# Six instead of four seven-product pairs in three of the four down projections, with half of the weight sums made by adding transfers

## The chip, the cores and the metric

The kernel runs on one core of a Trainium2 chip. The metric is the device time of one execution in microseconds (us), as the median of three runs.

## The reference

A two-block network on 256 tokens of width 1024 in fp32. The first block has four feed-forward layers (two per depth), a state-space mixer (SSD), a neighbourhood attention and two gated embeddings; the second has three attentions and a wide MLP. The change touches the feed-forward layers:

```python
def swiglu(x, w_gu, w_down):
    g, u = jnp.split(x @ w_gu, 2, axis=-1)
    return (jax.nn.silu(g) * u) @ w_down          # (256 x 2816) @ (2816 x 1024)

for i in range(DEPTH):                            # DEPTH = 2
    h = h + 0.5 * swiglu(rmsnorm(h, ffn1_norm[i]), ffn1_w_gu[i], ffn1_w_down[i])
    h = h + mixer_i(rmsnorm(h, mix_norm[i]))      # i = 0: SSD, i = 1: neighbourhood attention
    h = h + 0.5 * swiglu(rmsnorm(h, ffn2_norm[i]), ffn2_w_gu[i], ffn2_w_down[i])
    gate = jax.nn.sigmoid(rmsnorm(h, ple_norm[i]) @ ple_w_gate[i])
    h = h + gate * rmsnorm(p[i] @ ple_w_proj[i], ple_post_norm[i])
```

## The kernel before, in words

**Products.** Every fp32 operand is split into a high part and a low rest (`whi`, `wlo` of the weights, `aThi`, `aTlo` of the activations), and a product of two blocks is three matmuls: high by high, high by low, low by high. A matmul of the down projection takes a stationary 128 x 128 block (128 tokens, 128 of the 2816 inner features) and streams 512 weight columns. So the 22 feature blocks, two token halves and two column halves cost 22 x 4 x 3 matmuls if all is done plainly.

**Pairs.** Two feature blocks, two token halves and two column halves are eight block products. For a *pair* (feature blocks 2j and 2j+1) the kernel does them with seven (a Strassen-like scheme with sums of weight blocks and differences of activation blocks): 21 matmuls instead of 24. Before, each of the four layers (i = 0 to 3) has four pairs, j = 0 to 3 (`PAIRS`, line 21).

**Tiles.** Weights come in tiles, and a plan (`plan_of`, with `down_tiles` for the order of the down projection) lists them in the order in which all engines take them. In this document the tiles of a down projection are called:

- **P**j, label `paired`: two feature blocks by 1024 columns, loaded (1 MB); 1536 of its 2048 columns per partition are split, and TensorE does 9 matmuls with it;
- **M**j, label `mixed`: the four sums of weight blocks (2048 columns), not loaded; VectorE makes them out of the raw tile of P (`sums`: one addition over 1024 columns, then two over 512, each of which needs the last), and TensorE does 12 matmuls;
- **R**0, R1, ...: a `rest` tile, done plainly: four feature blocks of one column half, 24 matmuls, or two (1024 columns, 12 matmuls);
- **L**0, L1, L2: the last three tiles (24, 24 and 12 matmuls).

Before, the order is R0 P0 M0 R1 P1 M1 R2 P2 M2 R3 P3 M3 R4 L0 L1 L2; R4 is a short one. The 22 tiles of the up projection, two for each of 11 chunks c, come ahead of it.

**The ring of a tile.** SyncE loads it into one of four raw slots (`NRAW`), when the tile four loads before has been split. ScalarE writes `whi` (line 1546), VectorE then `wlo` (line 2130), into one of three slots (`NSPL`): tile n can be split only when TensorE has released tile n-3. TensorE takes tile n (`take`) when its `whi` and its `wlo` are there. `whi` of an M tile waits for the last of its sums. All engines follow one program order; VectorE's order in the down projection is sums of P, `wlo` of P, `wlo` of M, `wlo` of the next tile (`ahead`).

**Activations.** After up chunk c, TensorE turns its result (line 628), ScalarE copies it (`araw`, `aThi`), and for c below `PAIRS` GpSimd makes the differences (`differences`, line 2790: `dsum`, three operations); ScalarE and VectorE split them into `dThi` and `dTlo`. GpSimd has little else to do: reciprocal roots, a few additions of `h`, sums in the SSD mixer. It issues no transfer.

Of the kernel before, what the change touches and what calls it, by code (L numbers as in the profile page):

```python
# [20 lines left out]
PAIRS = 4  # L21
# [141 lines left out]
def plan_of(dr):  # L163
    p = Plan()

    def ffn(i, up, down, extra=None):
# [6 lines left out]
        def rest(c, y):  # L173
            k0, nk = DOWN_TILES[c, y]
            p.add(("down", i, c, y), [wsrc(down, k0, nk, c * 512, 512)], nk, 512)

        for what, x in DOWN_ORDER:
# [5 lines left out]
        for x in DOWN_LAST:  # L183
            rest(*x)
# [78 lines left out]
DOWN_ORDER, DOWN_TILES, DOWN_LAST = down_tiles(PAIRS)  # L263
# [130 lines left out]
def programs(dr, mem, banks, plan, ev):  # L394
# [33 lines left out]
    def landed(n):  # L428

        if labels[n][0] == "mixed":  # L430
            return at("tsum", *labels[n][1:])
        return at(f"d_w{plan.raw_of[n] % NRAW}", n)

    def dTlo(c):
        return mem["dTlo"][:, c, :, :]
# [117 lines left out]
    def sync(S):  # L553
# [67 lines left out]
    def tensor(T):  # L621
# [203 lines left out]
        def mixed_down(i, r, turn_last):  # L825
# [17 lines left out]
            def rest(c, y):  # L843
                k0, nk = DOWN_TILES[c, y]
# [10 lines left out]
            def seven(j):  # L855
                first, final = j == 0, j == PAIRS - 1
# [19 lines left out]
            for what, x in DOWN_ORDER[1:]:  # L876
# [6 lines left out]
            closing_block([("down", i) + DOWN_LAST[0]], (6, 7), aThi, aTlo, DOWN_TILES[DOWN_LAST[0]][0])  # L883
            residual_in(r, 0, (6, 7))
            held, k0 = [], DOWN_TILES[DOWN_LAST[1]][0]
            for x in DOWN_LAST[1:]:
                hi, lo = take("down", i, *x)
                held += [(hi[:, k, :], lo[:, k, :]) for k in range(DOWN_TILES[x][1])]
            T.wait_ge(*at("aTlo", i, 10))
            for t in range(2):  # L890
                for k, (hi, lo) in enumerate(held):
# [7 lines left out]
                    if t and k == DOWN_TILES[DOWN_LAST[1]][1] - 1:  # L899
                        last.then_inc(*sig(*named(("down", i) + DOWN_LAST[1])))  # L900
                last.then_inc(*sig(*half(("down", i) + DOWN_LAST[2], t)))
# [637 lines left out]
    def scalar(A):  # L1539
# [71 lines left out]
        def ffn(i, r, extra=None):  # L1611
            fa, aThi = mem["fa"], mem["aThi"]

            def high_a(c):
                A.wait_ge(*at("turn_a", i, c))
                b = banks[4 + c % 2]
                if c >= PAIRS:
# [15 lines left out]
            def mixed_down(r):  # L1633
                take("down", i, 0, 0)
                high_a(10)
                for what, x in DOWN_ORDER[1:]:
# [14 lines left out]
                take("down", i, *DOWN_LAST[2])  # L1651
# [6 lines left out]
            for c in range(11):  # L1658
# [15 lines left out]
                if 1 <= c <= PAIRS:  # L1674
# [451 lines left out]
    def vector(V):  # L2126
# [8 lines left out]
        def sums(n):  # L2135
# [9 lines left out]
            else:  # L2145
                V.wait_ge(*at("dTlo", i, PAIRS - 1))
# [914 lines left out]
```

## Time and profile before

| | |
|---|---|
| median of three runs | 1669.83 us (1669.68 to 1669.99) |
| the profiled execution | 1669.54 us |
| its span (first to last instruction) | 1667.7 us |
| TensorE (PE) busy | 1655.8 us, 99% |
| VectorE (DVE) busy | 1161.4 us, 70% |
| ScalarE (ACT) busy | 940.5 us, 56% |
| GpSimd (POOL) busy | 125.1 us, 8% |
| transfers | 300.58 MB, mean 180 GB/s |

The profiler's span is 1.84 us shorter than the time of the same execution; differences between two spans can be added to the time as they are. "Busy" is an average over stages; whether VectorE is early or late for one tile is read from a timeline. A matmul's duration in a row is the time from its start to the end of its pipeline, so the pace of TensorE is read from starts, or from a piece of the chain divided by its matmuls.

### The profile page before, as it was taken

How to read it: one execution, taken by the hardware profiler on the slowest of the kernel's cores; microseconds unless marked ns; L12 is line 12 of the kernel's file. 1: busy time of each engine (PE TensorE's matmuls, PEld its weight loads, DVE VectorE, ACT ScalarE, POOL GpSimd, SP SyncE). 2: the span in 40 equal slices, each digit the busy share in tenths (PEclk: the TensorE clock that was granted, in tenths of full speed). 3: DMA queues.
4: the chain of work that ended last, by engine and by line, in shares of the span. 5: the costliest groups of instructions: out<-in, count | busy, mean ns of one | idle time of the engine just before them, and what ended most of it. 6: DMA issues, size and time to landing. Idle time of an engine off the chain costs nothing.

```text
span 1667.7 us, 23289 instructions
## 1 busy us (share of the span) xinstructions
PE 1655.8 (99%) x9318; PEld 1416.7 (85%) x9318; DVE 1161.4 (70%) x1500; ACT 940.5 (56%) x1363; POOL 125.1 (8%) x135
## 2 busy tenths in 40 slices
PE   8999999999999999999999999999999999999998
PEld 7888899999788888888888778888889999988886
DVE  5657878999966568765688767567855578776643
ACT  6545566777865445754456666545653556564532
POOL 0100000000111000010007401000000000000000
PEclk9999999999999999999999999999999999999999
DMA  9654677676556646656487336655655533465551
GB/s 302 194 183 164 186 187 208 180 196 207 161 190 197 195 158 204 200 178 194 159 228 244 114 111 205 190 184 163 220 182 165 161 102 127 156 210 178 177 195 57
DMA packets 244235, 300.58 MB, mean 180 GB/s; under 512 B 9505, under 2 KB 175777, under 8 KB 244129
## 3 DMA queue, kind: packets, MB, share of 16 engines
q1 hardware_dynamic: 238480, 289.26, 54.6%
q10 hardware_dynamic: 5648, 9.85, 2.4%
q8 instruction: 74, 1.21, 0.3%
q14 instruction: 33, 0.26, 0.0%
HBM read 297.96 MB, written 1.11 MB: 179 GB/s over the span
## 4 chain that ended last, share of the span: by engine, by line
PE 98%; DVE 1%; DMA 0%; ACT 0%; issue 0%; DVEq 0%; ACTq 0%
PE bank L625 95%; PE bank L628 4%; DMA prm<-in_prm 0%; DVE wlo L2130 0%; ACT hThi L1546 0%; DVE rTlo L2133 0%; DVE hTlo L2133 0%; DVE xn L2133 0%; DVE h L2133 0%; ACT rThi L1546 0%; DVE xn L2200 0%; DVEq L2988 0%; ACT xn L1543 0%; ACT whi L1546 0%; ACTq L2086 0%
## 5 line engine op out<-in xcount | busy, mean ns | idle before, releaser
L2130 DVE TENSOR_TENSOR wlo<-raw,whi 128x2048 fp32r<-128x2048 f32 (+2 forms) x284 | 613.5, 2165 | 231.1 <-ACT whi L1546 231.1
L1546 ACT ACTIVATE whi<-raw 128x2048 fp32r<-128x2048 f32 (+2 forms) x284 | 511.7, 1810 | 167.1 <-PE bank L625 162.7
L625 PE MATMUL bank<-whi,hThi 128*128 128x512 f32 x1056 | 420.8, 398 | 0.5 <-ACT whi L1546 0.5
L625 PE MATMUL bank<-wlo,hThi 128*128 128x512 f32 x1056 | 412.4, 390 | 0.4 <-DVE wlo L2130 0.4
L625 PE MATMUL bank<-whi,hTlo 128*128 128x512 f32 x1056 | 396.9, 391 | 0.0
L625 PE MATMUL bank<-hThi,whi 128*128 128x256 f32 x888 | 253.4, 285 | 0.0
L625 PE MATMUL bank<-hThi,wlo 128*128 128x256 f32 x888 | 251.2, 283 | 0.0
L625 PE MATMUL bank<-hTlo,whi 128*128 128x256 f32 x888 | 251.2, 283 | 0.0
L625 PEld LDWEIGHTS bank<-whi,hThi 128*128 128x128 f32 x1056 | 198.8, 188 | 44.8 <-issue 5.8
L625 PEld LDWEIGHTS bank<-whi,hTlo 128*128 128x128 f32 x1056 | 198.6, 188 | 42.4
L625 PEld LDWEIGHTS bank<-wlo,hThi 128*128 128x128 f32 x1056 | 198.8, 188 | 40.3 <-DVE wlo L2130 1.5
L625 PEld LDWEIGHTS bank<-hThi,whi 128*128 128x128 f32 x888 | 169.5, 191 | 3.8 <-issue 3.3
L625 PEld LDWEIGHTS bank<-hTlo,whi 128*128 128x128 f32 x888 | 169.5, 191 | 0.2
L625 PEld LDWEIGHTS bank<-hThi,wlo 128*128 128x128 f32 x888 | 169.5, 191 | 0.2
L625 PE MATMUL bank<-whi,aThi 128*128 128x512 f32 x288 | 113.6, 395 | 0.4
L625 PE MATMUL bank<-whi,aTlo 128*128 128x512 f32 x288 | 112.2, 390 | 0.0
L625 PE MATMUL bank<-wlo,aThi 128*128 128x512 f32 x288 | 112.1, 389 | 0.0
L1543 ACT ACTIVATE ftmp<-bank,st 128x256 f32<-128x256 f32 x88 | 41.5, 476 | 101.5 <-PE bank L625 101.5
L2130 DVE TENSOR_TENSOR aTlo<-bank,aThi 128x512 fp32r<-128x512 f32 (+2 forms) x60 | 29.3, 511 | 78.5 <-ACT aThi L1546 78.5
L1546 ACT ACTIVATE aThi<-bank 128x512 fp32r<-128x512 f32 (+2 forms) x60 | 25.5, 457 | 98.3 <-PE bank L628 98.3
L2790 POOL TENSOR_TENSOR st<-st,cst 128x1 f32<-128x1 f32 (+2 forms) x35 | 36.9, 1068 | 458.6 <-DVE st L2173 433.5
L1546 ACT ACTIVATE hThi<-bank,prm 128x128 fp32r<-128x128 f32 (+1 forms) x152 | 43.4, 379 | 47.5 <-PE bank L628 42.4
(245 smaller groups left out, 2157.0 us busy)
## 6 DMA issues: line engine op xcount, KB each, us to landing
raw<-in_ffn_w_gu SPq DMA_DIRECT2D x172, 512.0 KB, 4.8
raw<-in_w_in SPq DMA_DIRECT2D x30, 1024.0 KB, 5.1
raw<-in_ffn_w_down SPq DMA_DIRECT2D x24, 1024.0 KB, 5.1
raw<-in_ffn_w_down SPq DMA_DIRECT2D x40, 512.0 KB, 4.0
raw<-in_ssd_w_in SPq DMA_DIRECT2D x16, 1024.0 KB, 5.7
raw<-in_ssd_w_in SPq DMA_DIRECT2D x32, 512.0 KB, 5.6
raw<-in_w_up SPq DMA_DIRECT2D x16, 1024.0 KB, 5.4
raw<-in_w_down SPq DMA_DIRECT2D x16, 1024.0 KB, 5.1
```

Source lines behind the costliest of these rows:

```text
L625: return T.e.matmul(out, lhsT, rhs, start=start, stop=stop, skip_group_check=skip)
L628: return T.e.transpose(out, in_, ident)
L1543: return e.activation(out, in_, func, **kw)
L1546: return e.activation(out, in_, ACT.Identity, **kw)
L2130: return e.tensor_tensor(out, a, b, op)
L2790: return e.tensor_tensor(out, a, b, op)
```

## The change

- Layers i = 1, 2, 3 get six pairs; layer 0 keeps four. For six pairs `down_tiles` gives the order R0 P0 M0 R1 P1 M1 R2 P2 M2 P3 M3 P4 M4 P5 M5 L0 L1 L2, where R2 is the short one (12 matmuls): four pairs stand directly behind each other.
- For the pairs 1, 3 and 5 of these layers (`AHEAD`), VectorE makes no sums. M1, M3 and M5 are loaded from a DRAM buffer `mix` (1 MB each) through a raw slot of their own, and P1, P3 and P5 load three quarters (0.75 MB), without the block that only the sums need.
- `mix` is filled by 54 transfers (nine tiles of six steps) on GpSimd's queue, from DRAM to DRAM: three of six copy, three add (`accum_op`). They move 512 KB (steps 0 and 1) or 256 KB each. Each waits for the one before (`m_step`) and for a weight tile's `whi` (`mix_at`), so at most one is under way. They are set one per up chunk (two tiles) in the feed-forward layers and one per two projection tiles in the SSD mixer. None is issued in a down projection.
- The differences are made for six chunks in these layers; `dTlo` is cut in two buffers.

```diff
--- before.py
+++ after.py
@@ -18,7 +18,11 @@
-PAIRS = 4
+PAIRS = (4, 6, 6, 6)
+AHEAD = ((), (1, 3, 5), (1, 3, 5), (1, 3, 5))
+BEATS = (range(1, 11), range(11), range(10), range(10))
+SSD_BEATS = (1, 29, 2)
+MIX = [(i, j) for i in range(4) for j in AHEAD[i]]
@@ plan_of: the mixed tile of a pair in AHEAD now has a source in DRAM
-                p.add(("mixed", i, x), None, 4, 512)
+                p.add(("mixed", i, x), [dr["mix"][i, x]] if x in AHEAD[i] else None, 4, 512)
@@ each layer has an order of its own
-DOWN_ORDER, DOWN_TILES, DOWN_LAST = down_tiles(PAIRS)
+DOWN_ORDER, DOWN_TILES, DOWN_LAST = zip(*(down_tiles(n) for n in PAIRS))
...
+    def summed_here(n):
+        return labels[n][0] == "mixed" and labels[n][2] not in AHEAD[labels[n][1]]
...
@@ sync, load(n)
-                if labels[m][0] == "paired":
+                if labels[m][0] == "paired" and summed_here(m + 1):
                     S.wait_ge(*at("tsum", *labels[m][1:]))
+            if labels[n][0] == "paired" and not summed_here(n + 1):
+                e.dma_start(slot[:, 1:2, 0:512], pieces[0][:, 1:2, :]).then_inc(*sig(f"d_w{q % NRAW}", n, by=16))
+                e.dma_start(slot[:, :, 512:1024], pieces[1]).then_inc(*sig(f"d_w{q % NRAW}", n, by=16))
+                return
+            if labels[n][0] == "mixed":
+                S.wait_ge(*at("m_step", *labels[n][1:], 5))
...
@@ vector, ahead(m)
-                if labels[n][0] == "paired":
+                if labels[n][0] == "paired" and summed_here(n + 1):
                     sums(n)
...
@@ gpsimd
+        def mix(i, j, step):
+
+            w = dr["ffn1_w_down" if i % 2 == 0 else "ffn2_w_down"][i // 2]
+            block = lambda k, c: w[256 * j + 128 * k:256 * j + 128 * k + 128, 512 * c:512 * c + 512].unsqueeze(1)
+            first = block(0, 0)
+            diagonal = bass.AP(first.tensor, first.offset, [[D, P], [P * D + 512, 2], [1, 512]])
+            target = dr["mix"][i, j]
+            if step == 0:
+                done = e.dma_start(target[:, 0:2, :], block(0, 1).to_broadcast([P, 2, 512]))
+            elif step == 1:
+                done = e.dma_start(target[:, 0:2, :], diagonal, accum_op=ALU.add)
+            elif step == 2:
+                done = e.dma_start(target[:, 2:3, :], target[:, 0:1, :])
+            elif step == 3:
+                done = e.dma_start(target[:, 2:3, :], block(1, 1), accum_op=ALU.add)
+            elif step == 4:
+                done = e.dma_start(target[:, 3:4, :], target[:, 2:3, :])
+            else:
+                done = e.dma_start(target[:, 3:4, :], block(1, 0), accum_op=ALU.add)
+            done.then_inc(*sig("m_step", i, j, step, by=16))
+
+        steps = [(i, j, step) for i, j in MIX for step in range(6)]
+        beats = iter(range(len(steps)))
+
+        def mix_at(n):
+
+            b = next(beats, None)
+            if b is not None:
+                G.wait_ge(*at("w_hi", n))
+                if b:
+                    G.wait_ge(*at("m_step", *steps[b - 1]))
+                mix(*steps[b])
+
         def ffn(i, extra=None):
-            for c in range(PAIRS):
-                differences(i, c)
+
+            for c in range(11):
+                if c < PAIRS[i]:
+                    differences(i, c)
                 if c == 2 and extra is not None:
                     ple_rstd(extra)
+                if c in BEATS[i]:
+                    mix_at(tile["up", i, c, 0])
...
         rstds(1)
+        for k in range(*SSD_BEATS):
+            mix_at(tile[SSD_TILES[k]])
         ssd()
...
@@ layout and build
-    put("dThi", [P, PAIRS, 3, P], F32R, a0)
-    put("dTlo", [P, PAIRS, 3, P], F32R, z + 56 * 1024)
+    put("dThi", [P, 7, 3, P], F32R, a0)
+    put("dTloA", [P, 5, 3, P], F32R, z + 56 * 1024)
+    put("dTloB", [P, 2, 3, P], F32R, z + 72 * 1024)
...
+    dr["mix"] = nc.dram_tensor("mix", (4, 7, P, 4, 512), F32, kind="Internal").ap()
```

VectorE, the down projection of layer i = 1, before, from `aTlo` of the last chunk on. `wlo<-raw` over 2048 columns is an R tile, over 1536 a P tile, over 1024 a short R tile; `ts` are the sums, and `wlo<-ts` is an M tile.

```order
L2130 TENSOR_TENSOR wlo<-raw,whi 128x2048 [waits s_w_hi]
L2130 TENSOR_TENSOR ts_75<-raw 128x1024 [waits s_w_rel,s_d_w2]
L2130 TENSOR_TENSOR ts_75<-ts_75,raw 128x512 [waits s_v_sums] x2
L2130 TENSOR_TENSOR wlo<-raw,whi 128x1536 [waits s_w_hi]
L2130 TENSOR_TENSOR wlo<-ts_75,whi 128x2048 [waits s_w_hi]
L2130 TENSOR_TENSOR wlo<-raw,whi 128x2048 [waits s_w_hi]
L2130 TENSOR_TENSOR ts_76<-raw 128x1024 [waits s_d_w0]
L2130 TENSOR_TENSOR ts_76<-ts_76,raw 128x512 [waits s_v_sums] x2
L2130 TENSOR_TENSOR wlo<-raw,whi 128x1536 [waits s_w_hi]
L2130 TENSOR_TENSOR wlo<-ts_76,whi 128x2048 [waits s_w_hi]
```

The same engine and layer of the changed kernel, from R2 (1024 columns) to P5; M3 is `wlo<-raw` over 2048 columns now:

```order
L2143 TENSOR_TENSOR wlo<-raw,whi 128x1024 [waits s_w_hi]
L2143 TENSOR_TENSOR ts_76<-raw 128x1024 [waits s_w_rel,s_d_w1]
L2143 TENSOR_TENSOR ts_76<-ts_76,raw 128x512 [waits s_v_sums] x2
L2143 TENSOR_TENSOR wlo<-raw,whi 128x1536 [waits s_w_hi]
L2143 TENSOR_TENSOR wlo<-ts_76,whi 128x2048 [waits s_w_hi]
L2143 TENSOR_TENSOR wlo<-raw,whi 128x1536 [waits s_w_hi]
L2143 TENSOR_TENSOR wlo<-raw,whi 128x2048 [waits s_w_hi]
L2143 TENSOR_TENSOR ts_75<-raw 128x1024 [waits s_w_lo,s_d_w0]
L2143 TENSOR_TENSOR ts_75<-ts_75,raw 128x512 [waits s_v_sums] x2
L2143 TENSOR_TENSOR wlo<-raw,whi 128x1536 [waits s_w_hi]
L2143 TENSOR_TENSOR wlo<-ts_75,whi 128x2048 [waits s_w_hi]
L2143 TENSOR_TENSOR wlo<-raw,whi 128x1536 [waits s_w_hi]
```

Between the sums of P2 and those of P4 stand four `wlo`, of P2, M2, P3 and M3, and no R tile; before, an R tile stood between any two pairs.

GpSimd in the up projection of layer i = 1, before: differences of the chunks 1 and 2 and two roots.

```order
L2790 TENSOR_TENSOR dsum<-araw 128x256 [waits s_araw]
L2790 TENSOR_TENSOR dsum<-araw,dsum 128x128 [waits s_g_differences] x2
L2790 TENSOR_TENSOR dsum<-araw 128x256 [waits s_dTlo,s_araw]
L2790 TENSOR_TENSOR dsum<-araw,dsum 128x128 [waits s_g_differences] x2
L2790 TENSOR_TENSOR st<-st,cst 128x1 [waits s_v_gates] x2
```

And now:

```order
L2803 TENSOR_TENSOR dsum<-araw 128x256 [waits s_araw]
L2803 TENSOR_TENSOR dsum<-araw,dsum 128x128 [waits s_g_differences] x2
L2896 DMA mix<-in_ffn_w_down 128x2x512 [waits s_m_step,s_w_hi]
L2803 TENSOR_TENSOR dsum<-araw 128x256 [waits s_dTlo,s_araw]
L2803 TENSOR_TENSOR dsum<-araw,dsum 128x128 [waits s_g_differences] x2
L2803 TENSOR_TENSOR st<-st,cst 128x1 [waits s_v_gates] x2
L2898 DMA mix<-mix 128x512 [waits s_m_step,s_w_hi]
```

A step, with its wait for the step before, now stands between the differences of two chunks.

## Rows read from the trace of the kernel before

**Rows 1.** The page: span, busy time, and the chain that ended last, by engine

```profile
span 1667.7 us, 23289 instructions
...
PE 1655.8 (99%) x9318; PEld 1416.7 (85%) x9318; DVE 1161.4 (70%) x1500; ACT 940.5 (56%) x1363; POOL 125.1 (8%) x135
...
PE 98%; DVE 1%; DMA 0%; ACT 0%; issue 0%; DVEq 0%; ACTq 0%
```

**Rows 2.** The chain in order of time (start, us, piece), down projections of i=1 and 3

```profile
597.70 10.93 PE bank L625 x48
...
609.07 4.79 PE bank L625 x21
...
613.98 41.13 PE bank L625 x180
...
1132.28 41.09 PE bank L625 x180
```

**Rows 3.** TensorE's timeline (start, us, instruction) at the start of R1, i=1

```profile
613.98 0.47 PE L625 MATMUL bank<-whi,aThi 128*128 128x512 f32 x1
614.29 0.39 PE L625 MATMUL bank<-wlo,aThi 128*128 128x512 f32 x1
```

**Rows 4.** VectorE's timeline, down projection of i=1: R1, P1, M1, R2, R4

```profile
611.54 2.29 DVE L2130 TENSOR_TENSOR wlo<-raw,whi 128x2048 fp32r<-128x2048 f32 x1 [1.11 <-ACT whi L1546]
613.75 1.22 DVE L2130 TENSOR_TENSOR ts<-raw 128x1024 f32<-128x1024 f32 x1
615.00 1.42 DVE L2130 TENSOR_TENSOR ts<-ts,raw 128x512 f32<-128x512 f32 x2
616.34 1.75 DVE L2130 TENSOR_TENSOR wlo<-raw,whi 128x1536 fp32r<-128x1536 f32 x1
618.41 2.29 DVE L2130 TENSOR_TENSOR wlo<-ts,whi 128x2048 fp32r<-128x2048 f32 x1 [0.32 <-ACT whi L1546]
621.75 2.29 DVE L2130 TENSOR_TENSOR wlo<-raw,whi 128x2048 fp32r<-128x2048 f32 x1 [1.05 <-ACT whi L1546]
...
641.34 1.23 DVE L2130 TENSOR_TENSOR wlo<-raw,whi 128x1024 fp32r<-128x1024 f32 x1 [0.20 <-ACT whi L1546]
```

**Rows 5.** ScalarE's timeline in the same down projection: M1, then R2 with P2, R4

```profile
616.45 1.92 ACT L1546 ACTIVATE whi<-ts 128x2048 fp32r<-128x2048 f32 x1 [3.57 <-DVE ts L2130]
619.80 3.54 ACT L1546 ACTIVATE whi<-raw 128x2048 fp32r<-128x2048 f32 x2 [1.43 <-PE bank L625]
...
640.25 1.06 ACT L1546 ACTIVATE whi<-raw 128x1024 fp32r<-128x1024 f32 x1 [1.43 <-PE bank L625]
```

**Rows 6.** Transfers: issues by line, KB each, median us from issue to landing

```profile
raw<-in_ffn_w_down SPq DMA_DIRECT2D x24, 1024.0 KB, 5.1
...
cum<-ct ACTq DMA_DIRECT2D x1, 64.0 KB, 2.4
```

**Rows 7.** Loads into raw, two in a row (649 to 651 us)

```profile
L570 SPq DMA_DIRECT2D raw<-in_ple_w_gate x2: 367/368/368, 649.3 to 650.5; - x2
...
DMA to landing us min/median/max: 5.0/5.9/6.8
```

**Rows 8.** Stretches: window, us, busy by engine, clock, DMA share, GB/s

```profile
645.00:650.00 5.00, 5.00 (x24) 4.14 (x23) 4.57 (x3) 3.46 (x3) 0.00 (x0) 1.00 0.83 290
...
360.00:404.00 44.00, 44.00 (x365) 42.94 (x364) 43.09 (x70) 31.48 (x52) 0.00 (x0) 1.00 0.63 195
```

**Rows 9.** GpSimd's timeline in up chunks of i=1

```profile
507.50 0.73 POOL L2790 TENSOR_TENSOR dsum<-araw 128x256 f32<-128x256 f32 x1 [12.24 <-ACT araw L1546]
508.32 1.01 POOL L2790 TENSOR_TENSOR dsum<-araw,dsum 128x128 f32<-128x128 f32 x2
518.87 0.74 POOL L2790 TENSOR_TENSOR dsum<-araw 128x256 f32<-128x256 f32 x1 [9.55 <-ACT araw L1546]
```

**Rows 10.** ScalarE's timeline there: the differences are taken

```profile
512.69 0.30 ACT L1546 ACTIVATE aThi<-dsum 128x128 fp32r<-128x128 f32 x1
```

**Rows 11.** VectorE on xTs and gate (min/median/max ns), SSD stage

```profile
L2130 DVE TENSOR_TENSOR xTs<-xTs,gate x8: 691/692/884, 298.3 to 459.9; 128x512 f32<-128x512 f32 x8
```

More of the change, by code:

```diff
@@ L173, in rest @@
         def rest(c, y):
-            k0, nk = DOWN_TILES[c, y]
+            k0, nk = DOWN_TILES[i][c, y]
             p.add(("down", i, c, y), [wsrc(down, k0, nk, c * 512, 512)], nk, 512)
-        for what, x in DOWN_ORDER:
+        for what, x in DOWN_ORDER[i]:
             if what == "rest":
@@ L434, in dTlo @@
     def dTlo(c):
-        return mem["dTlo"][:, c, :, :]
+        return mem["dTloA"][:, c, :, :] if c < 5 else mem["dTloB"][:, c - 5, :, :]
     def rstd(r, t):
@@ L875, in mixed_down @@
             clear(0, 1, 2, 3, 5)
-            for what, x in DOWN_ORDER[1:]:
+            for what, x in DOWN_ORDER[i][1:]:
                 if what == "rest":
@@ L898, in mixed_down @@
                         turn(1, 0, 1)
-                    if t and k == DOWN_TILES[DOWN_LAST[1]][1] - 1:
-                        last.then_inc(*sig(*named(("down", i) + DOWN_LAST[1])))
-                last.then_inc(*sig(*half(("down", i) + DOWN_LAST[2], t)))
+                    if t and k == DOWN_TILES[i][DOWN_LAST[i][1]][1] - 1:
+                        last.then_inc(*sig(*named(("down", i) + DOWN_LAST[i][1])))
+                last.then_inc(*sig(*half(("down", i) + DOWN_LAST[i][2], t)))
             residual_in(r, 1, (2, 3))
@@ L1635, in mixed_down @@
                 high_a(10)
-                for what, x in DOWN_ORDER[1:]:
+                for what, x in DOWN_ORDER[i][1:]:
                     if what == "rest":
@@ L1650, in mixed_down @@
                     high(1, 0, 1)
-                take("down", i, *DOWN_LAST[2])
+                take("down", i, *DOWN_LAST[i][2])
                 if r == 1:
@@ L2253, in mixed_down @@
                 low_a(10)
-                for what, x in DOWN_ORDER[1:]:
+                for what, x in DOWN_ORDER[i][1:]:
                     if what == "rest":
@@ L2259, in mixed_down @@
                     take("mixed", i, x)
-                take("down", i, *DOWN_LAST[0])
+                take("down", i, *DOWN_LAST[i][0])
                 merged()
@@ L2263, in mixed_down @@
                 for t in range(2):
-                    residual(r, t, 0, half(("down", i) + DOWN_LAST[0], t), 6 + t, 0.5)
-                take("down", i, *DOWN_LAST[1])
+                    residual(r, t, 0, half(("down", i) + DOWN_LAST[i][0], t), 6 + t, 0.5)
+                take("down", i, *DOWN_LAST[i][1])
                 early_quarters(r)
@@ L2268, in mixed_down @@
                 for t in range(2):
-                    residual(r, t, 1, half(("down", i) + DOWN_LAST[2], t), 2 + t, 0.5)
+                    residual(r, t, 1, half(("down", i) + DOWN_LAST[i][2], t), 2 + t, 0.5)
                     if r == 1 and t == 0:
@@ L2274, in mixed_down @@
                     scaled(0)
-                take("down", i, *DOWN_LAST[2])
+                take("down", i, *DOWN_LAST[i][2])
                 if r == 1:
@@ L2896, in gpsimd @@
         ffn(3, 1)
+        assert next(beats, None) is None
         rstds(7)
```

38 lines of the change are left out of this document (19 added, 19 removed).

## The prediction

> **What bounds the kernel now.** I read the page first: the span is 1667.7 us, TensorE is busy for 1655.8 us of it, and the chain that ended last is TensorE's to 98% [rows 1]. So matmuls that go are worth their full time, unless TensorE waits for something in their place. Then the chain in order of time, at the down projection of layer i = 1. 48 matmuls over 512 columns take 10.93 us, so one takes 0.2277 us: P 2.05 us, M 2.73, a pair 4.78 (the row says 4.79 for 21), R 5.46, a short R 2.73. R0 and the first pair end at 613.86, and from 613.98 on 180 matmuls follow without a gap; in layer 3 the same [rows 2]. Last, VectorE's and ScalarE's timelines there, for the steps that lead from a released slot to the next tile:
>
> - release to `whi`: R1 begins at 613.98, ends 5.46 later at 619.44, and ScalarE begins R2's `whi` at 619.80: 0.36 us [rows 2, 5];
> - `whi` over 2048 columns 1.92 us, and VectorE begins 0.04 after it ends (616.45 + 1.92 = 618.37, then 618.41) [rows 4, 5];
> - `wlo` over 2048 columns: 2.29 to its end, 2.21 to the next start (611.54 to 613.75); over 1536 columns 1.75; sums: 2.59 to the next start (613.75 to 616.34), their last ends 0.08 after that (615.00 + 1.42), and M's `whi` begins 0.03 later [rows 4, 5];
> - `wlo` ended to TensorE started: 613.83 to 613.98, 0.15 us [rows 3, 4].
>
> A tile over 2048 columns thus needs 0.36 + 1.92 + 0.04 + 2.29 + 0.15 = 4.76 us from the release of the slot three tiles back, and TensorE spends 4.78 us on the two tiles between when these are a P and an M. R2 shows it: ready at 621.75 + 2.29 + 0.15 = 624.19, wanted at 619.44 + 4.78 = 624.22. The down projection runs without a gap, but with 0.03 us to spare; one rest tile between two pairs (5.46 us) is what lets VectorE catch up with the sums.
>
> **The change part by part.**
>
> *Removed matmuls.* Two more pairs in three layers, three matmuls less for each: 6 x 3 x 0.2277 = 4.10 us off TensorE's path.
>
> *VectorE where four pairs stand together (P2 to M5).* TensorE needs 4 x 4.78 = 19.1 us. VectorE needs 2.59 + 1.75 + 2.21 = 6.55 for a pair that it sums and 3.96 for one that is loaded, 21.0 together. It is short by 1.9 us, in spite of the loaded sums. Tile by tile:
>
> - M2: from R1's release 0.36 + 1.06 (`whi` over 1024 [rows 5]) + 0.03 + 1.15 (the short `wlo`, 1.23 to its end [rows 4], less the same 0.08 overlap) + 2.67 (sums) + 0.03 + 1.92 + 0.04 + 2.29 + 0.15 = 9.70; TensorE has P1, M1, R2 and P2, 9.56. It waits 0.14.
> - M3: 4.76 against M2 and P3, 4.78. No wait.
> - P4: its sums stand on VectorE behind `wlo` of M3, which waits for the release of P2. So 0.36 + 1.92 + 0.04 + 2.21 + 2.59 + 1.75 + 0.15 = 9.02, against M2, P3 and M3, 7.51: 1.51, of which M2's wait has taken 0.14. It waits 1.37. Queued behind these sums are `wlo` of P4 and M4, and TensorE wants both.
> - M4: counted from the start of P4's `wlo`: 0.08 + 0.03 + 1.92 + 0.04 + 2.29 + 0.15 = 4.51, and TensorE comes at 1.75 + 0.15 + 2.05 = 3.95. It waits 0.56.
> - P5, M5, L0: P5 is loaded and has 1 us to spare; M5 and L0 are the 4.76 against 4.78. No wait.
>
> 2.07 us per down projection, near the 1.9 of the balance; three give 6.21. A wait also breaks the stream: R1's second matmul comes 0.31 after its first instead of 0.23 [rows 3]. Nine restarts at 0.08 are 0.7 us. R1's own wait is there now too.
>
> *Loads.* A pair with loaded sums fetches 1.75 MB. From the issue of P2's load (R1 just split) to the `whi` of L0 the queue must bring 6.5 MB (6.8 million bytes). TensorE spends 5.46 + 4.78 + 2.73 + 3 x 4.78 and 2.07 of waits on the way, 29.4 us, 29.9 with the two handovers; less the fixed part of a load (5.1 less 3.0, below) 27.8 remain: 245 GB/s is needed. Two loads issued at 649.3 and 650.5 landed 5.0 and 6.8 us later, so 3.0 us apart: 350 GB/s [rows 7]; a 5 us stretch shows 290 [rows 8]. The tightest is P2: issued at 613.83 in R1's terms, landed 5.1 later [rows 6], wanted by its sums at 619.44 + 0.36 + 1.06 + 0.03 + 1.15 = 622.04, 3.1 us spare. Cost nothing; from 245 GB/s down it costs (rival C). The Trainium skill (DMA: Bandwidth & Descriptors, "Where 436 GB/s comes from") has about 358 GB/s of HBM bandwidth per core; a pair with loaded sums alone asks for 384 over its 4.78 us, so by that rule the ring has to carry part of it, as above, and the 350 measured agrees.
>
> *The 54 steps.* No row shows a transfer issued by GpSimd, nor one that adds. Below, the nearest row is the store of 64 KB to DRAM, 2.4 us; above, step 1 moves its 512 KB three times (both sources, then the result): 1 MB at 5.1 and the next 0.5 at 3.0 per MB are 6.6, plus 2.4 for the DRAM end, 9.0 us [rows 6, 7]. A step has an up chunk, 609.07 - 597.70 = 11.37 us [rows 2]. So the next step finds it done. The issue is hidden too: GpSimd ends the differences at 509.33 and is idle to 518.87, and ScalarE takes them at 512.69, 3.4 us after they are there [rows 9, 10]. The weight loads have four slots, so a few us of contention on the way change nothing in an up projection. I take 0. In the SSD mixer VectorE is busy for 43.09 of 44 us while TensorE has no gap [rows 8]; there 14 steps could disturb it. The longest of eight additions there is 0.19 above their median [rows 11]: at most 14 x 0.19 = 2.7 us, at least 0. I take 0, since nothing ties the transfers to VectorE.
>
> *Differences of chunks 4 and 5.* GpSimd has 9.5 idle us per chunk for them, and nobody needs them before the down projection. 0. The two added issues on SyncE's queue per loaded pair fall in its idle time.
>
> **Sum.** -4.10 + 6.21 + 0.72 = +2.8 us. The profiled execution took 1669.54 us, 1.84 above its span, and 0.29 below the median; the difference is put on the median: 1669.83 + 2.8 = 1672.7 us. A measurement of this kernel tells a change from none at about 0.2%, 3.3 us: 1666.5 to 1673.2.
>
> **Rivals.**
>
> *B, the gain arrives.* If TensorE is served in time among the four pairs, 1669.83 - 4.1 = 1665.7. For it: the trace shows TensorE never stopped by more than 0.12 in a down projection although spare time is 0.03. Against: the 9.02 us of P4's path are sums of durations that repeat in each down projection, in an order that VectorE cannot change; all 1.5 us would have to go. A half-way case (P4 waits 0.7, nothing else does, one restart) is -4.1 + 3 x 0.78: 1668.1.
>
> *C, slower, by the loads.* The place is L0, behind 6.5 MB of loads. It decides below 245 GB/s. At 220 the loads take 31.0 us instead of 27.8: 3.2 us per down projection, 9.6 together, 1682. For it: the mean over the span is far lower than 245, and 1.75 MB per pair has not been asked for before. Against: 350 and 290 GB/s, and no step is under way in a down projection.
>
> *D, slower, by a step that outlasts its beat.* GpSimd then waits for `m_step` ahead of the next differences, ScalarE's `dThi` waits for these, and the `whi` behind it. Covered are the 3.4 us at ScalarE and what a tile has to spare in an up projection (two tiles of 5.46 less 4.76, 6.2): 9.6 in five chunks, so it decides from 11.37 + 1.9 = 13.3 us per step. At 16 the lag of 4.6 us a chunk is 23 at chunk 5, 13.5 not covered, three times: about 1713. The Trainium skill (SBUF — State Buffer, "SBUF: two separate sides", the box on the "DVE blocks DMA" trap) says that VectorE in a two-port mode keeps GpSimd from writing the descriptors of its transfers, which would lengthen a step. It names copies and the like; VectorE's rows here are additions and subtractions of two tensors, and no run here shows the rule.
>
> *E, the same waits, somewhat dearer.* The 4.76 against 4.78 stands at three places per down projection (M3, M5, L0). If VectorE or ScalarE is 0.1 us slower on that path, each costs 0.08 and P4 0.1 more: 0.35 per layer, 1 us. With the SSD bound of 2.7 this reaches 1676.4.
>
> **Chances.** The forecast with its own range of 1670.5 to 1674.5: 60%. E beyond that: 12%. B 6%, half-way 8%. C 9%. D 5%. Range for 8 in 10: 1668.3 to 1677. Faster by over 0.2% (below 1666.5): 8%. Slower by over 0.2% (above 1673.2): C, D and E, 26%, and the part of the forecast's own range above that, 13%: 39%. Faster takes in B and the lower end of the half-way case. Within 0.2%: 53%.
>
> **What would show it.** Right: in the chain of the three down projections pieces of about 1.4 us before P4 and 0.6 before M4, released by `wlo` on VectorE, 18 matmuls less, the first layer unchanged, and the up projections at 11.37 a chunk. Wrong: TensorE without gaps from R1 to L2 (B); `sums` or `whi` of P4, M5 or L0 waiting for a landing (C); GpSimd waiting for a transfer and `dThi` late (D); VectorE rows longer than 2.29 (E).

## The result, and the profile after

The changed kernel takes 1674.59 us (median of 7 runs, 1674.05 to 1675.73); the kernel before, timed beside it, 1669.68 us (7 runs, 1668.97 to 1670.96). The ratio is 1.0032 with a 95% interval of 1.002 to 1.0043, so it is 4.9 us slower, by the interval 3.3 to 7.2. The forecast was 1672.7, slower by 2.8. The profiled execution took 1675.41 us.

The page of the changed kernel, against [rows 1]: the span, the engines and the chain.

```profile
span 1673.6 us, 23465 instructions
...
PE 1655.1 (99%) x9300; PEld 1413.7 (84%) x9300; DVE 1167.7 (70%) x1515; ACT 955.4 (57%) x1393; POOL 177.4 (11%) x207
...
PE 96%; DVE 2%; ACT 1%; issue 1%; DMA 0%; ACTq 0%; DVEq 0%
```

18 matmuls are gone (9318 to 9300), and the chain has lost two points of TensorE to VectorE, ScalarE and "issue". Where, the chain in order of time says (start, us, piece; after, down projection of i=1, against [rows 2]):

```profile
600.29 10.93 PE bank L638 x48
...
611.66 4.79 PE bank L638 x21
...
616.57 15.24 PE bank L638 x66
...
631.89 1.93 ACT whi L1559
...
633.87 2.17 issue
636.05 1.23 DVE ts L2143
...
638.75 1.92 ACT whi L1559
...
640.70 2.30 DVE wlo L2143
...
643.14 15.23 PE bank L638 x66
```

Before, 180 matmuls ran from 613.98 to 655.11, 41.13 us. Now TensorE's work from R1 to the end is two pieces of 66 matmuls with `whi` of M3, the sums of P4, `whi` and `wlo` of M4 between: 616.57 to 658.37, 41.80 us. Six matmuls less (174), and 0.7 us more. VectorE's timeline shows the order of this (after, same place, P3 to M4, against [rows 4]; in brackets the idle time before and who ended it):

```profile
631.47 1.75 DVE L2143 TENSOR_TENSOR wlo<-raw,whi 128x1536 fp32r<-128x1536 f32 x1
633.84 2.29 DVE L2143 TENSOR_TENSOR wlo<-raw,whi 128x2048 fp32r<-128x2048 f32 x1 [0.61 <-ACT whi L1559]
636.05 1.22 DVE L2143 TENSOR_TENSOR ts<-raw 128x1024 f32<-128x1024 f32 x1
637.30 1.42 DVE L2143 TENSOR_TENSOR ts<-ts,raw 128x512 f32<-128x512 f32 x2
638.64 1.75 DVE L2143 TENSOR_TENSOR wlo<-raw,whi 128x1536 fp32r<-128x1536 f32 x1
640.70 2.29 DVE L2143 TENSOR_TENSOR wlo<-ts,whi 128x2048 fp32r<-128x2048 f32 x1 [0.31 <-ACT whi L1559]
```

The durations are those of before to 0.01 us. The sums of P4 start at 636.05, right behind `wlo` of M3, as forecast. TensorE's timeline has the stop before P4 (after; the row before it starts at 639.06):

```profile
639.06 0.39 PE L638 MATMUL bank<-whi,aTlo 128*128 128x512 f32 x1
640.49 0.47 PE L638 MATMUL bank<-whi,aThi 128*128 128x512 f32 x1 [1.05 <-issue]
```

640.49 - 639.06 - 0.23 = 1.20 us for P4. Read the same way, M4 waits 0.49 and M2 0.07. Layers 2 and 3 repeat it: two pieces of 66 matmuls with 11.3 us from the end of one to the start of the next; there R1 to the end takes 0.75 us more than before.

The SSD mixer also lost time. The chain there, of before and then of after:

```profile
205.53 29.56 PE bank L625 x244
235.09 0.03 issue
235.12 24.58 PE bank L625 x200
```

```profile
206.88 29.56 PE bank L638 x244
236.44 1.27 issue
237.71 24.58 PE bank L638 x200
```

The same matmuls, and a stop of 1.27 us instead of 0.03. "issue" says only that the profile shows no releaser; ScalarE's timeline does (before, then after; `ACTq` is the issue of a transfer):

```profile
227.41 0.34 ACTq L1766 DMA_DIRECT2D cum<-ct  x1
...
230.77 1.92 ACT L1546 ACTIVATE whi<-raw 128x2048 fp32r<-128x2048 f32 x1 [3.40 <-DMA cum<-ct]
```

```profile
228.75 0.34 ACTq L1779 DMA_DIRECT2D cum<-ct  x1
...
233.37 1.92 ACT L1559 ACTIVATE whi<-raw 128x2048 fp32r<-128x2048 f32 x1 [4.65 <-DMA cum<-ct]
```

ScalarE stores 64 KB, issues the two transfers that read them back when the store has landed, and the next `whi` stands behind these issues: 3.36 us from the store's issue to `whi` before, 4.62 after. The store took 2.4 us before and now 3.6. Around it (windows of after, then of before at the same work; the last two numbers are the DMA engines' busy share and GB/s):

```profile
223.35:225.35 2.00, 2.00 (x17) 1.79 (x17) 2.00 (x6) 0.79 (x1) 0.00 (x0) 1.00 0.97 100
225.35:227.35 2.00, 2.00 (x19) 2.00 (x18) 2.00 (x5) 0.82 (x3) 0.00 (x0) 1.00 0.75 144
```

```profile
222.00:224.00 2.00, 2.00 (x17) 1.79 (x17) 2.00 (x6) 0.79 (x1) 0.00 (x0) 1.00 0.12 16
224.00:226.00 2.00, 2.00 (x19) 2.00 (x18) 2.00 (x5) 0.81 (x3) 0.00 (x0) 1.00 0.98 271
```

An adding step (256 KB, issued at 221.74, landed at 228.12) keeps the DMA engines 97% busy at 100 GB/s, where before they were 12% busy. In the next two microseconds, with the step and two weight loads under way, they move 144 GB/s; before, the two loads alone had 271. The loads land later, and the store comes into their tail.

By stage, from the first `dsum` of each layer, `gate` of the SSD mixer and the additions to `h` in both timelines, the 5.9 us between the two spans are: first loads 1.35, SSD mixer 1.24, the three down projections 2.59 (0.7 each up to the turn behind them, and 0.1 more right behind it), the rest of the middle 0.07, the end 0.65.

The end is not the last stores: they land 2.1 us after their issue in both. It is GpSimd's last instruction (`DRAIN`), for which all engines wait at the end of the program (before, then after; count, ns min/median/max, start):

```profile
L2988 POOLq DRAIN  x1: 1089/1089/1089, 1662.6 to 1662.6; - x1
```

```profile
L3042 POOLq DRAIN  x1: 5522/5522/5522, 1667.8 to 1667.8; - x1
```

Before it was long over when the last store landed, and the span ended 0.40 us behind that landing; now it ends 0.79 us behind it, and the span 1.02. It takes 5.52 us in each of the seven kernels here that issue steps (after, e1, e3, e5, e6, e8, e9), and 1.09 in each of the five that don't; from TensorE's last matmul to the end of the span the first take 7.53 us and the others 6.9 to 7.1. So the steps cost 0.6 us at the end, whenever they are issued.

The first loads: in the four profiles of kernels with four pairs (before, e5, e7, e10) GpSimd's first difference starts at 29.5 to 30.0 us, in the eight with six pairs at 29.6 (e8) to 31.3, seven of them at 30.3 or later. The medians are 0.8 us apart. No run shows why, and one profile each can't divide it from scatter; the profiled execution of after lies 0.8 above the median of its kernel.

The steps themselves (issues by line: count, KB, median us to landing; after):

```profile
mix<-in_ffn_w_down POOLq DMA_DIRECT2D x18, 512.0 KB, 7.5
...
mix<-mix POOLq DMA_DIRECT2D x18, 256.0 KB, 4.7
mix<-in_ffn_w_down POOLq DMA_DIRECT2D x18, 256.0 KB, 6.3
```

The first row mixes two steps: by line, step 0 (a copy) has a median of 5.5 us and step 1 (adding) 8.7, against the 9.0 of the estimate for it. The longest of all 54 took 10.0, under the 11.37 of the beat. GpSimd's waits (what it waited for, us in total, times, longest) show that all 22 chunks' differences waited for `araw`, as in [rows 9], and none for a step:

```profile
POOL dsum L2803 <- ACT araw L1559: 200.9, 22, 14.3
```

Of the 54 issues 15 did wait for the step before, up to 9.9 us, where GpSimd came to several beats late and issued them back to back; no difference was late by it.

### The profile page after: what moved, and what is told of

The parts are those of the page before. It is cut to its first block, busy times and chain, and to the rows that moved or that the text cites. A ratio compares the mean times of both kernels' runs of the same rounds, so it can differ in the third digit from the quotient of the medians.

```text
span 1673.6 us, 23465 instructions
## 1 busy us (share of the span) xinstructions
PE 1655.1 (99%) x9300; PEld 1413.7 (84%) x9300; DVE 1167.7 (70%) x1515; ACT 955.4 (57%) x1393; POOL 177.4 (11%) x207
## 4 chain that ended last, share of the span: by engine, by line
PE 96%; DVE 2%; ACT 1%; issue 1%; DMA 0%; ACTq 0%; DVEq 0%
PE bank L638 92%; PE bank L641 4%; ACT whi L1559 1%; DVE wlo L2143 1%; DVE ts L2143 0%; DMA h<-in_x 0%; DVE rTlo L2146 0%; DVE hTlo L2146 0%; DVE xn L2146 0%; DVE h L2146 0%; ACT rThi L1559 0%; ACT hThi L1559 0%; DVE xn L2213 0%; DVEq L3042 0%; ACT xn L1556 0%
## 5 line engine op out<-in xcount | busy, mean ns | idle before, releaser
L2143 DVE TENSOR_TENSOR wlo<-raw,whi 128x2048 fp32r<-128x2048 f32 (+3 forms) x293 | 630.2, 2157 | 233.0 <-ACT whi L1559 233.0
L1559 ACT ACTIVATE whi<-raw 128x2048 fp32r<-128x2048 f32 (+3 forms) x293 | 526.8, 1805 | 181.1 <-PE bank L638 175.3
L638 PE MATMUL bank<-whi,aThi 128*128 128x512 f32 x264 | 104.5, 396 | 3.6 <-issue 3.2
L638 PE MATMUL bank<-whi,aTlo 128*128 128x512 f32 x264 | 102.9, 390 | 0.0
L638 PE MATMUL bank<-wlo,aThi 128*128 128x512 f32 x264 | 102.8, 389 | 0.0
L2143 DVE TENSOR_TENSOR aTlo<-bank,aThi 128x256 fp32r<-128x256 f32 (+2 forms) x66 | 28.9, 466 | 77.4 <-ACT aThi L1559 77.4
L1559 ACT ACTIVATE aThi<-bank 128x256 fp32r<-128x256 f32 (+2 forms) x66 | 25.2, 420 | 76.7 <-PE bank L641 76.7
```

The source lines that it names most:

```text
L638: return T.e.matmul(out, lhsT, rhs, start=start, stop=stop, skip_group_check=skip)
L1559: return e.activation(out, in_, ACT.Identity, **kw)
L2143: return e.tensor_tensor(out, a, b, op)
```

## The experiments

The kernel before was timed in each series beside them; its medians were 1669.5 to 1669.9. "Ratio" is against it.

**e7, the scale and the start.** The kernel before under another name.

> The kernel before, once more, for the beginning of its profile: the first activations of ScalarE wait there for the load of x or of the parameters, and the changed kernels so far reached the first differences on GpSimd 0.7 to 1.35 us later than the kernel before. If the load varies from run to run, this profile lies among them (30.0 to 31.3 us); if the changed kernels are slower there by themselves, it is at 30.0 again.

Measured: 1669.32 us (1668.62 to 1670.58, 10 runs), ratio 0.9998 (0.9989 to 1.0007). Differences below about 1.5 us say nothing in one series. Its first difference starts at 29.86 us, which is the second case of the expectation: the later start seems to belong to the changed kernels. e8, at 29.59, speaks against it. Its SSD mixer takes 0.2 us less than in the profile of before, so 0.2 us there is scatter.

**e4, are the waits VectorE's sums?** All sums back on VectorE, no steps and no loaded sums, six pairs kept:

```diff
-AHEAD = ((), (1, 3, 5), (1, 3, 5), (1, 3, 5))
+AHEAD = ((), (), (), ())
```

> The changed kernel with six pairs and all sums on VectorE, no steps, no loaded sums. Theory V: P3, P4 and P5 each wait 1.4 to 1.5 us and M3, M4 and M5 0.5 each, with 0.1 for M2 and seven restarts of 0.08 about 6.7 us of waits per down projection, so 5.3 longer each: 1669.7 + 16 = about 1686 (with the P4 and M4 waits as measured, 1.2 and 0.5, 1683). Theory L: no steps and fewer loads, so 4 us faster than before.

Measured: 1685.26 us (1684.05 to 1686.44, 4 runs), ratio 1.0092 (1.0078 to 1.0106). In the profile the chain goes through the sums of P2, P3, P4 and P5 (i=1; e4):

```profile
623.02 1.15 DVE ts L2143
...
629.80 1.23 DVE ts L2143
...
636.66 1.23 DVE ts L2143
...
643.52 1.23 DVE ts L2143
```

The first row is the sums of P2. From P3 on they are 6.86 us apart (2.71 for the sums, 1.94 for `whi` of M, 2.21 for its `wlo`), where TensorE needs 4.78 for a pair. Its stops are 1.40, 1.37 and 1.39 before P3, P4, P5 and 0.49 to 0.52 before M3, M4, M5, where the arithmetic of the prediction gives 1.5 and 0.55. The whole, 15.4 us slower than before, is near the 16 expected. The sum model holds in another configuration than the one that it was made for.

**e2, everything but the steps.** The steps are not issued, and the three mixed tiles are loaded from weights in the place of sums:

```diff
-MIX = [(i, j) for i in range(4) for j in AHEAD[i]]
+MIX = []
-                p.add(("mixed", i, x), [dr["mix"][i, x]] if x in AHEAD[i] else None, 4, 512)
+                p.add(("mixed", i, x), [wsrc(down, 2 * x, 4, 0, 512)] if x in AHEAD[i] else None, 4, 512)
-            if labels[n][0] == "mixed":
-                S.wait_ge(*at("m_step", *labels[n][1:], 5))
```

> The changed kernel without the 54 steps: GpSimd issues no transfer, and M1, M3, M5 are loaded from four plain blocks of the weights (1 MB as well), so the products with them are not the reference's. Theory V: the down projections keep their waits (1.2 before P4, 0.5 before M4) and stay 0.7 us longer than before, the gap of 1.3 us in the SSD mixer goes: 1.3 below the changed kernel, +2 to +3.6 on the kernel before. Theory L: all the loss goes and the three matmuls per pair arrive, -4 us on the kernel before.

Measured: 1672.68 us (1671.74 to 1673.71, 11 runs), ratio 1.0017 (1.0008 to 1.0026): +2.8. The down projections show the waits of after (2.6 us for the three), the SSD mixer takes what it takes before (0.2 less), and GpSimd's `DRAIN` is at 1.09 us again. That the time is the forecast's sum to 0.1 us is in part chance: the profile also has the later start.

**e5, the steps alone.** Four pairs as before, VectorE's sums, and all 54 steps issued, with a result that nobody uses:

```diff
-PAIRS = (4, 6, 6, 6)
-AHEAD = ((), (1, 3, 5), (1, 3, 5), (1, 3, 5))
+PAIRS = (4, 4, 4, 4)
+AHEAD = ((), (), (), ())
-MIX = [(i, j) for i in range(4) for j in AHEAD[i]]
+MIX = [(i, j) for i in (1, 2, 3) for j in (1, 3, 5)]
```

> Four pairs in every layer as in the kernel before, all sums on VectorE, and the 54 steps issued at their places, their result used by nothing. Theory S (the steps cost only what the store of cum loses behind them): 1.3 us on the kernel before, all of it between the first SSD tile and the store, 1671. Rival (the steps cost in the up projections and the SSD mixer generally, by contention or by GpSimd): more than 2 us, spread over the stages.

Measured: 1671.86 us (1671.53 to 1673.37, 11 runs), ratio 1.0015 (1.0006 to 1.0023): +2.4 (1.0 to 3.8). That is more than the 1.3 of theory S, but it is not spread as the rival has it. In its profile the SSD mixer has lost 1.57 us and the end 0.6 (the `DRAIN`); layers 1 and 2 take what they take before to 0.04, and the down projection of i=1 is one piece of 41.12 us. e2 and e5 together give 5.2, against the 4.9 of the change.

**e3, one beat left out.** The step beside the store is issued one beat (two projection tiles) later, and so are those behind it:

```diff
-        for k in range(*SSD_BEATS):
+        for k in (1, *range(5, 30, 2)):
```

> The changed kernel with one beat of the SSD mixer left out (the step issued ahead of the store of cum), the later ones each one place earlier in the list of steps. Theory S (an adding step delays the raw loads, these the store of cum, ScalarE waits for that store with whi queued behind it, and TensorE stops for 1.27 us at 236): the gap goes, 1.3 us off the changed kernel, 1673.3. Rival (the store is slower by chance in that execution): the gap comes and goes, the time stays at 1674.6.

Measured: 1673.07 us (1671.91 to 1674.04, 11 runs), ratio 1.0019 (1.001 to 1.0028): 1.5 less than the changed kernel, which is no more than the noise between two series. The profile decides: the chain has no stop there (e3), and `whi` comes 3.02 us after the store's issue:

```profile
206.47 53.91 PE bank L638 x444
```

So of 54 steps one costs time where it is issued, 1.2 us (1.6 in e5), because a store that everything waits for is under way behind it. The `DRAIN` at the end is still 5.52 us here.

**e1, other pairs loaded.** P3, P4 and P5 get the loaded sums, so that VectorE has none among the four:

```diff
-AHEAD = ((), (1, 3, 5), (1, 3, 5), (1, 3, 5))
+AHEAD = ((), (3, 4, 5), (3, 4, 5), (3, 4, 5))
```

> The changed kernel with the same number of loaded sums and steps, for the pairs 3, 4 and 5 instead of 1, 3 and 5: no pair that VectorE sums stands among the last four but P2. Theory V (TensorE waits because the sums of P4 stand on VectorE behind wlo of M3): the waits before P4 and M4 go, that before M2 (0.1 us) stays; each down projection is then 1.37 - 0.2 shorter than in the kernel before instead of 0.7 longer, and with the 1.3 us in the SSD mixer the whole is 2 us faster than before, 1667.5 to 1669. Theory L (the waits come from transfers: the steps, or the loads of 1.75 MB per pair): the same number of steps and three heavy pairs in a row, so at least the 1674.6 of the changed kernel, and waits for landings in the last three pairs.

Measured: 1674.69 us (1671.47 to 1679.08, 6 runs), ratio 1.0029 (1.0017 to 1.004). No gain, which was the miss. VectorE's waits are gone, and loads stand in their place (chain, then ScalarE's timeline, i=1; e1):

```profile
640.25 6.59 DMA raw<-in_ffn_w_down
```

```profile
644.17 1.92 ACT L1559 ACTIVATE whi<-raw 128x2048 fp32r<-128x2048 f32 x1 [1.54 <-DMA raw<-in_ffn_w_down]
646.86 1.92 ACT L1559 ACTIVATE whi<-raw 128x2048 fp32r<-128x2048 f32 x1 [0.77 <-DMA raw<-in_ffn_w_down]
```

`whi` of L0 and L1 wait for landings of 6.6 to 6.9 us, and TensorE stops 0.57 us before L0 and 0.69 before the turn behind the projection. This is rival C's place, three loaded pairs in a row, which take two of the four raw slots each. L0's load is issued at 637.25, when P4 has been split, and ScalarE is free for it at 642.63: 5.4 us, and it took 6.9. From R1 to the turn it gains nothing: 41.17 us against before's 41.13. The same profile stops 0.9 and 0.6 us in layer 2, 2.0 in layer 3, and 1.7 at the third load of the attention, of which e6 tells more.

**e8, the same with less to load.** e1 with only two of the four blocks of each mixed tile loaded (its sums are thus incomplete):

```diff
-AHEAD = ((), (1, 3, 5), (1, 3, 5), (1, 3, 5))
+AHEAD = ((), (3, 4, 5), (3, 4, 5), (3, 4, 5))
+                e.dma_start(slot[:, 0:2, :], pieces[0][:, 0:2, :]).then_inc(*sig(f"d_w{q % NRAW}", n, by=16))
+                return
```

> The run with loaded sums for the pairs 3, 4 and 5, where the loads of M3, M4 and M5 fetch two of their four blocks only (0.5 MB instead of 1), so the products with them are not the reference's. Theory (in that run the last three tiles waited for their loads, which four raw slots start too late for three heavy pairs in a row): the landings come 1.5 us earlier, the waits before M5 and L0 and the late turn at the end of the down projection go, each is 1.2 us shorter than in the kernel before, and the whole is 3 to 6 us faster than that run, 1669 or less. Rival (something else in that order costs the time, such as ScalarE or VectorE being late with the last tiles): no faster than 1674.

Measured: 1671.34 us (1669.09 to 1678.6, 12 runs), ratio 1.0017 (1.0008 to 1.0025). 3.3 us less than e1, but not the 1669 expected. The profile does not bear out the reason either: `whi` of L0 waits for its landing longer than in e1 (e8, i=1):

```profile
643.10 1.92 ACT L1561 ACTIVATE whi<-raw 128x2048 fp32r<-128x2048 f32 x1 [1.85 <-DMA raw<-in_ffn_w_down]
```

L0's load took 7.2 us there against 6.9 in e1, and TensorE stops 0.86 us before L0 and 1.05 at the turn. In layer 3 of the same profile, with the same order and loads, it took 5.2 us and nothing stopped. So a load of 1 MB lands there after 5 to 7 us, whatever stands ahead of it, and the lead of 5.4 us is too short for the longer ones; what makes one long isn't shown. Nor is it shown that the bytes are what makes e8 faster than e1: its profile has no stop at the attention and starts 1.1 us sooner. Single executions of both lie 4 to 7 us above their medians.

**e6, the pairs spread.** An R tile is moved between P2 and the pairs behind it, the last two pairs are loaded, and the beat of e3 is left out. The order is R0 P0 P1 R1 P2 R2 P3 P4 P5 (each P with its M):

```diff
-AHEAD = ((), (1, 3, 5), (1, 3, 5), (1, 3, 5))
+AHEAD = ((), (1, 4, 5), (1, 4, 5), (1, 4, 5))
@@ down_tiles
-        if others:
+        if others and not (pairs == 6 and j == 0):
@@ gpsimd
-        for k in range(*SSD_BEATS):
+        for k in (1, *range(5, 30, 2)):
```

> The changed kernel with order R0 P0 P1 R1 P2 R2 P3 P4 P5, loaded sums for the pairs 1, 4 and 5, and the beat ahead of the store of cum left out. Theory V with the limit of the loads: VectorE gets a rest tile before P2 and the short one before P3, the only pairs that it sums behind others, and no more than two loaded pairs stand together; waits per down projection at most 0.2 us, each 1.2 to 1.4 shorter than in the kernel before, nothing lost in the SSD mixer: 1669.7 - 3.9 = 1665.5 to 1666.5, the fastest of all. Rival (six pairs cannot be fed in any order; the loads of P4 to L0 are late as in the run with the pairs 3, 4 and 5): 1669 or more, with waits of ScalarE for landings before L0.

Measured: 1669.63 us, but 1665.02 to 1674.39 over 12 runs; ratio 1.0002 (0.9991 to 1.0013). The down projections do what was asked (chain, i=3; e6):

```profile
1131.85 44.50 PE bank L638 x195
```

No stop in 195 matmuls; before took 4.79 + 0.12 + 41.09 = 46.0 us for the 201 of this stretch. 1.5 us less is what six matmuls (1.37) and a restart are worth, and three of it should have given 1665. In the profiled execution (1673.3 us) a new stop took it back, in the attention, where nothing was edited (chain, e6; `SPq` is SyncE issuing a transfer, L589 is `pT`):

```profile
857.46 5.44 SPq L589
...
863.57 16.47 DMA raw<-in_na_w_qkv
...
884.44 13.79 PE bank L638 x48
```

SyncE issues the table of the neighbourhood attention (two transfers of 1000 KB from `in_rpb` in small pieces), which waits for the last M tile of layer 2, then `pT` and `row`, then the third qkv load. Behind the table's small pieces the issue of `pT` takes 5.4 us, and the load lands 16.5 us after its issue. Before, the same load was issued at 863.31, 0.26 us sooner, took 13.8, and was in time by about 1 us, with TensorE 2.6 us behind where it is in e6. Counted from TensorE's place the load is issued 2.9 us later in e6. 0.5 of it is the table's own wait, for a last M tile with no short R tile behind it; the rest is SyncE's issues, 3.2 and 5.4 us instead of 1.2 and 5.0. Why these are longer isn't shown.

The stop itself is 4.6 us, from 879.8 to 884.4. In it the granted clock of TensorE falls to 0.50, its lower level of 1.2 GHz, and stays there until about 890 (e6; the third number from the end):

```profile
886.00:888.00 2.00, 2.00 (x7) 1.54 (x6) 1.97 (x4) 1.54 (x1) 0.21 (x1) 0.50 0.92 346
```

Matmuls start 0.43 us apart there instead of 0.23. 48 matmuls that took 11.1 us before take 18.3: the stop costs 4.5 us by itself and 2.6 more by the clock. Stops of up to 2.0 us (e1, e4, e8, e9) had no such fall behind them. That fits the scatter of e6's runs, 9 us wide, though only one of them has a profile.

**e9, the load ahead of the table.** e6 with two moves in SyncE's program:

```diff
-            if n == tile["qkv", NA_CHUNKS[1], 0]:
+            if n == tile["qkv", NA_CHUNKS[1], 1]:
                 table()
+            if n == tile["qkv", NA_CHUNKS[5], 1]:
                 pos(1)
```

> The kernel of e6_spread, with the table of the neighbourhood attention (the two in_rpb transfers, which wait for the last mixed tile of layer three) issued by SyncE one qkv load later, and pT and row of the second position embedding eight loads later. If the 4.5 us wait of TensorE at the third qkv load in e6's profile, and the scatter of its runs (1665.0 to 1674.4), come from that load standing behind the table and pT in SyncE's program and queue, then the third qkv load is issued before 860 us, TensorE doesn't wait for it, and what e6 gained stays: before's 1669.5 less 3 x 1.43 us of the down projections and less 0.24 in the SSD mixer = 1665.0, range 1664.0 to 1666.5, with runs within 2 us of each other. Rival: the small pieces of in_rpb hold back whichever load comes next, so the fourth qkv load is late instead: 1668 to 1670, scattered as e6. Second rival: the table now lands after GpSimd needs it (889.9 us in before) and the attention's biases wait: 1667 or more with a GpSimd wait on in_rpb.

Measured: 1666.82 us (1665.79 to 1667.75, 11 runs); before in the same series 1669.61 (21 runs). Ratio 0.9982 (0.9973 to 0.9991): 2.8 us faster than the kernel before, and 7.8 faster than the changed one (medians of different series). The scatter is 2 us. The attention's stop is gone, and the issue of `pT` takes 0.5 us (SyncE's timeline, e9):

```profile
856.83 4.10 SPq L597 DMA_DIRECT2D tb<-in_rpb  x2
861.04 42.02 SPq L583 DMA_DIRECT2D raw<-in_na_w_qkv  x8
903.11 0.50 SPq L589 DMA_DIRECT2D pT<-in_pT  x1
```

The first of the `x8` is the fourth qkv load, now the first behind the table: its issue takes 5.5 us and it lands 18.1 us after it, as the first rival has it, but TensorE doesn't wait for it. The table lands at 876.7 us, in time for GpSimd, so the second rival is out.

The time is 1.8 us short of the 1665.0 expected, and outside the range. By stage against before: SSD mixer -0.2, layers 2 and 3 -1.4 each, layer 1 only -0.45. There L1's load lands late (chain, i=1; e9), and TensorE stops 1.16 us before the turn:

```profile
638.43 6.51 DMA raw<-in_ffn_w_down
```

That is 1.0 of it. The same load, in the same order, took 5.07 us in e6, and layer 1 gained its 1.4 there, so this is scatter of a load with a lead of 5.3 us, and no property of two loaded pairs. In the profile 0.6 more is the `DRAIN` at the end, which the expectation had left out, and 0.6 the first loads.

**e10, the control.** The kernel before with the same two moves.

> The kernel before, with the same two moves in SyncE's program (table one qkv load later, pT and row eight loads later) and nothing else. In before's profile no instruction of TensorE waits for a qkv load at that place, so both theories of e9 expect no change: 1669.5, range 1668.5 to 1670.5. If it is faster by over 1 us, before too lost time there in its unprofiled runs, and what e9 gains over e6 is no property of the changed order; if it is slower, the table itself is what is needed first.

Measured: 1669.53 us (1668.96 to 1671.04, 11 runs), ratio 1.0 (0.9991 to 1.0009). The moves alone give nothing: before, the late load was covered.

## Why the prediction was right or wrong

The direction and the mechanism in the down projections were right, and the size was 2.1 us too small: +4.9 against +2.8. 1674.59 is inside the range for 8 in 10 and 0.1 above the forecast's own range.

One reading under the sum was off. It let R1 end at 619.44, 5.46 us after its start, and left out R1's own restart. The next tile's first matmul starts 0.1 later (before):

```profile
619.54 0.39 PE L625 MATMUL bank<-whi,aThi 128*128 128x512 f32 x1
```

So `whi` follows a release by 0.26 us, not 0.36, R2 was wanted at 624.30, and the down projection had 0.11 us to spare, not 0.03.

- *Removed matmuls, -4.10.* Right: 18 gone, and e6 and e9 show 1.4 per layer wherever nothing stops TensorE.
- *VectorE at P2 to M5, +6.21 and 0.72 for restarts.* The places are right, all three, and no other stops appear. The sizes are somewhat smaller: P4 1.20 (1.37), M4 0.49 (0.56), M2 0.07 (0.14), restarts 0.08 each. Up to the turn a layer costs 0.67 to 0.75, where the sum gave 0.94. Two slips of the sum are the difference: the 0.10 above, and restarts counted twice. Those of M2 and P4 lie in time in which TensorE would wait for the next tile anyway, and only M4's costs 0.08; 0.10 and 2 x 0.08 are 0.26 per layer. With 0.1 right behind the turn, which the sum lacks, the three layers cost 2.59, near the 2.8.
- *The 54 steps, 0.* This is the step that failed. The estimate of 9.0 us for step 1 was right (8.7). That the next step finds it done failed for 15 of the 54, without harm. But I bounded their cost in the SSD mixer by VectorE alone [rows 8, 11], "since nothing ties the transfers to VectorE", and took the weight loads' four slots as cover. The store `cum<-ct` has no slots: ScalarE stands still until it has landed, [rows 6] had its 2.4 us, and a wait of 3.4 us stood in the timeline of before. One step beside it costs 1.24 in the profile; e5 gives 2.4 (1.0 to 3.8) for all steps and e3 takes 1.5 back. The 1.24 is inside the bound of 2.7, for another reason than the bound's. The second cost, 0.6 us for GpSimd's `DRAIN`, is at the end of the program, where the prediction didn't look at all. The Trainium skill (DMA: Bandwidth & Descriptors, "Latency and other measured facts") says that a transfer's fixed cost is mostly HBM's latency and grows under load; the store's 2.4 to 3.6 us beside the step agrees, though no run here separates the latency from the engines being busy.
- *Loads, 0.* Right for the changed kernel, where no wait of the down projections is a landing. What rival C lacked is the lead of the issue. It decides by GB/s over the whole stretch, and the queue has these: the kernel before moves 383 to 387 GB/s from 872 to 880 us, more than the 350 that the prediction read from two loads, and e9 328 to 405 while its L1 is late. But one load has only 5.4 us between its issue and its use, and loads of 1 MB landed there after 4.9 to 7.3. In e1 that cost 0.6 to 0.7 us twice in layer 1, and in e9 1.0 in one layer.
- *Rivals.* B is out: P4's wait is there in each layer (e4 repeats it at three pairs). D is out by the steps' durations. E is out: no row of VectorE is longer.
- What is left of the 4.9: 2.6 for the down projections, 1.24 for the store and 0.6 for the `DRAIN` leave about 0.5 us. It may be the later start of the kernels with six pairs (0.8 between the medians of the profiles), whose cause no run shows; it stays open.
- *Slower by over 0.2%.* The forecast lay 0.5 us under that boundary (1673.2); the missing SSD term alone would have carried it over. So the likeliest case, a time within 0.2% (53%), is not what came, and the 39% is.

## What to carry to other kernels

Work that leaves a busy engine for the DMA queues is paid for by the transfers that someone stands still for: list these (a store that is read back, a load with a short lead) before asking for free bandwidth, and keep the new transfers off them. An engine that issued none before may also need longer to end the program. When sums or other extra work of an engine come with some tiles only, their order counts for more than their number: with four pairs in a row a down projection was 0.9 us longer than before, with the pairs spread 1.4 shorter. The whole went from 4.9 us slower to 2.8 faster, of which the step moved off the store is 1.2 to 1.5. And a local gain moves every release behind it, so look at what the next stage's queue issues on these releases: there e6 lost what it had gained.

## What was not expected of the hardware

- An adding transfer is expensive for its bytes: 256 KB take 6.3 us where a copy of 256 KB takes 4.7, and 512 KB take 8.7 where a copy takes 5.5. While one of 256 KB was under way the DMA engines were 97% busy at 100 GB/s; two weight loads had 271 GB/s at 98%.
- A kernel in which GpSimd issued transfers ends with a `DRAIN` of 5.52 us on GpSimd instead of 1.09, even when the last of its transfers landed 570 us before (after: at 1098.1).
- Issuing a transfer can block the issuing engine: the first transfer behind the table's two takes SyncE 3.9 to 6.5 us to issue, whether it is `pT` (before, after, e1, e6, e7) or a weight load (e9, e10), and `pT` takes 0.5 with no table ahead. While the table was moving (858 to 868 us in e6), the queue did 200 to 216 GB/s at full busy share, and loads behind it landed after 16.5 to 18.5 us instead of 5.
- After a stop of 4.6 us TensorE was granted 0.50 of its clock for about 5 us more (e6); after stops of up to 2.0 us it kept 1.00.
